# A hybrid decoder layer on one core: x and B of the SSD mixer turned by VectorE and DMA instead of TensorE

## The chip, the cores and the metric

The kernel runs on one core of a Trainium2 chip. The metric is the device time of one execution in microseconds (us). A comparison of this kernel can tell a difference of about 0.2%, some 5 us, from none.

## What is computed

One layer on 16 learned meta tokens and 2048 tokens of 1024 features, all in float32. `u`, `z`, `xBC` and `dt` are columns of one projection; x has 24 heads of 64 channels in 4 groups, B and C have 128 channels per group.

```python
def reference(x, meta, norm_mix_w, w_in, ...):
    h = concatenate([meta, x])
    hn = rms_norm(h, norm_mix_w)
    u, z, xbc, dt_raw = split(hn @ w_in)                 # 512, 1536, 2560, 24 columns
    y_pool = pool_mixer(u, pool_w, pool_scale)           # trailing means over 2, 4, 8, 16 tokens
    y_ssm = ssd_mixer(z, xbc, dt_raw, ...)
    h = h + concatenate([y_pool, y_ssm]) @ w_out
    h = h + square(relu(rms_norm(h, norm_ffn_w) @ w_ff1)) @ w_ff2
    return rms_norm(h, norm_f_w)[16:]

def ssd_mixer(...):                                      # per chunk of 128 tokens and group g
    x, B, C = silu(causal_dwconv(xbc))                   # width 4, over tokens
    y_diag = ((C @ B.T) * decay) @ (x * dt)
    state  = state * chunk_decay + B.T @ (decay_to_end * x * dt)
    y_off  = (C @ state_before) * exp(a_cs)
    y = (y_diag + y_off + d_skip * x) * silu(z)          # then a norm per group and ssm_norm_w
```

## The kernel before

The sequence is cut into 4 blocks of 512 tokens (`TB`). Block 0 splits each fp32 weight into a high and a low fp32r part (`high_part` on ScalarE, L541; `low_part`, L556, on VectorE in the mixer) and stores both in DRAM (`w_scr`); blocks 1 to 3 load them back. Every product is then three fp32r products. A block runs the input projection in items (`unit`, L1901), the mixer steps between them, and then the output projection. After the four blocks come the feed-forward products, from 1390 us to the end, which the change doesn't enter.

**Items.** An item is one tile of 128 channels by 512 tokens: per group g the tiles B (j=0), C (j=1) and three x tiles (j=2, 3, 4), then z: in block 0 three more tiles, in blocks 1 to 3 four pieces of one chunk each (`z_unit`, L1910). Last come four pool tiles. For each item TensorE makes the product into bank 0 or 1; ScalarE copies it out (`evac`, L1317); VectorE runs three convolution taps (`taps`, L2378), ScalarE a tanh, VectorE the SiLU product (`finish`, L2394), which writes `group_tile(g, j)` in feature order (channels on partitions). `evac(v)` waits until item v-2 is finished, and TensorE starts item v+2 only when `evac(v)` is done.

**Mixer steps.** Step q (16 in a block, four chunks c for each group) mixes group g while the items of group g+1 run; for the last group only one pool item runs in each step. In a step TensorE does: item n1, `y_transposes(q-2)`, `diagonal(q-1)` (L2023; it waits for `xw_ready(q-1)`), `slot1(q)`, `state(q-1)`, item n2, `y_offset(q)`. The mixer needs x and B of the chunk with tokens on partitions, so `slot1` (L1973) turns four 128x128 tiles on TensorE into bank 4 or 5 (L1985), ScalarE copies them to `xb` and `b_plain` or `b_both` (L1547, L1549), and GpSimd (`ty`, L1125) and VectorE (`xdt` L2583, `xw` L2587) read `xb`. VectorE's order in a step is: `y_finish`, `state_add` of the step before, taps of n1, in block 0 the low weight part of n1+2, the mask, the product with E, `xdt`, `xw`, low parts, the `finish` of two items, `yo`, in block 0 the low weight part of n2+2, taps of n2.

**Queues.** All DMAs are issued by SyncE in one written order. In the loop over n (L825) it issues, in block 0, the stores of the split weights of unit n-4 (which wait for the low part of that unit) and then the raw load of unit n; in blocks 1 to 3 it waits until unit n-4 or so is done and loads the two parts of unit n. Between them stand the store of the running totals (`store_sums`, L791) and the loads of their broadcasts (`load_sums`, L800), which ScalarE's exponentials need.

## Time and profile before

| | |
|---|---|
| median of 3 runs | 2673.69 us (2671.85 to 2674.07) |
| span of the profiled execution | 2674.7 us |
| busy TensorE, VectorE, ScalarE, GpSimd | 99%, 61%, 48%, 41% |
| granted TensorE clock, mean | 0.999 of full speed |

The span runs from the first to the last instruction and stands 1.0 us above the median, so a shift that is worked out in the span is applied to the median as it is. In the rows further down a timeline line has its start, its length (of all xcount instructions together), the engine and the source line, what is written and read, and in brackets the idle time before it with what ended it. "PE" is TensorE, "DVE" VectorE, "ACT" ScalarE, "POOL" GpSimd, "SPq" SyncE's queue.

### The profile page before, as it was taken

To read this page: it belongs to the slowest core of one execution; us is meant where nothing else is said; L and a number is where in the kernel's file an instruction comes from. 1 tells how busy PE (TensorE), PEld (TensorE's weight loads), DVE (VectorE), ACT (ScalarE), POOL (GpSimd) and SP (SyncE) were. 2 spreads that over 40 slices of the span, in tenths; PEclk is the share of its full clock that TensorE was granted. 3 is DMA by queue.
4 is the path that set the end of the run, shared out by engine and by line. 5 is a ranking of instruction groups with operands and counts; after the bars stand their busy time and mean duration, and the time that the engine had idled before them with its cause. 6 is when DMAs were issued, how large, how long until landed. Compare 5 with 4: busy or idle time off the path is not lost.

```text
span 2674.7 us, 37670 instructions
## 1 busy us (share of the span) xinstructions
PE 2654.5 (99%) x14058; PEld 2225.0 (83%) x14058; DVE 1636.3 (61%) x2204; ACT 1281.4 (48%) x2562; POOL 1091.7 (41%) x866
## 2 busy tenths in 40 slices
PE   8999999999999999999999999999999999999998
PEld 6788778888888888898888888888888888888887
DVE  6788714788136883367853576574445766666667
ACT  4577654666245672355734454555454322222223
POOL 2133440335003441023444688665554535353434
PEclk9999999999999999999999999999999999999999
DMA  9977676654646546555574555774445842423324
GB/s 327 299 255 244 237 247 223 251 181 172 220 174 245 194 160 236 190 215 181 188 267 142 200 197 203 259 259 154 152 151 207 309 145 96 164 103 126 118 95 157
DMA packets 224451, 531.14 MB, mean 199 GB/s; under 512 B 14074, under 2 KB 97022, under 8 KB 214798
## 3 DMA queue, kind: packets, MB, share of 16 engines
q1 hardware_dynamic: 224270, 528.74, 55.3%
q8 instruction: 112, 1.84, 0.3%
q14 instruction: 69, 0.57, 0.1%
HBM read 382.74 MB, written 145.95 MB: 198 GB/s over the span
## 4 chain that ended last, share of the span: by engine, by line
PE 95%; DMA 2%; SPq 1%; DVE 1%; issue 0%; POOL 0%; ACT 0%; POOLq 0%; ACTq 0%
PE bank L2257 23%; PE bank L2225 22%; PE bank L1832 21%; PE bank L1939 12%; PE bank L1919 7%; PE bank L2023 2%; PE bank L1985 1%; PE bank L2040 1%; PE bank L2003 1%; PE bank L2011 1%; DMA w_scr<-w_both 1%; DMA meta_w<-in_w_in 1%; PE bank L1991 1%; PE bank L1958 1%; DMA raw<-in_w_out 0%
## 5 line engine op out<-in xcount | busy, mean ns | idle before, releaser
L1832 PE MATMUL bank<-hnT_hi,w_ring 128*128 128x512 f32 x1152 | 369.4, 392 | 0.0
L2257 PE MATMUL bank<-w_first,T_hi 128*128 128x512 f32 x896 | 275.8, 389 | 0.0
L2387 DVE SCALAR_TENSOR_TENSOR acc<-pre,par,acc 128x512 f32<-128x512 f32 x240 | 211.6, 882 | 90.4 <-ACT pre L1345 84.6
L1832 PEld LDWEIGHTS bank<-hnT_hi,w_ring 128*128 128x128 f32 x1152 | 216.3, 188 | 44.5 <-ACT win_tmp L1474 0.5
L2742 DVE TENSOR_TENSOR acc_th<-bank,acc_th 128x512 f32<-128x512 f32 x224 | 150.0, 686 | 155.4 <-PE bank L2257 154.0
L2225 PE MATMUL bank<-T_hi,w_both 128*128 128x512 f32 x768 | 242.4, 389 | 0.5 <-DVE ff L2683 0.5
L1939 PE MATMUL bank<-w_ring,T_hi 128*128 128x512 f32 x768 | 239.0, 392 | 0.1
L1832 PE MATMUL bank<-hnT_lo,w_ring 128*128 128x512 f32 x576 | 224.5, 390 | 0.0
L2257 PEld LDWEIGHTS bank<-w_first,T_hi 128*128 128x128 f32 x896 | 168.2, 188 | 34.9
L1919 PE MATMUL bank<-w_ring,hnT_hi 128*128 128x384 f32 x768 | 196.0, 336 | 0.0
L1832 PE MATMUL bank<-hnT_hi,w_both 128*128 128x512 f32 x544 | 183.1, 408 | 2.3 <-ACT pre L1345 2.3
L2225 PE MATMUL bank<-b,w_both 128*128 128x512 f32 x768 | 179.5, 389 | 0.0
L2257 PE MATMUL bank<-T_hi 128*128 128x512 f32 x448 | 174.3, 389 | 0.0
L2257 PE MATMUL bank<-T_lo,T_hi 128*128 128x512 f32 x448 | 174.3, 389 | 0.0
L2257 PE MATMUL bank<-w_first,T_lo 128*128 128x512 f32 x448 | 174.3, 389 | 0.0
L2257 PE MATMUL bank<-T_hi,T_lo 128*128 128x512 f32 x448 | 174.3, 389 | 0.0
L2225 PEld LDWEIGHTS bank<-T_hi,w_both 128*128 128x128 f32 x768 | 144.1, 188 | 31.2 <-DVE ff L2683 1.3
L2225 PEld LDWEIGHTS bank<-b,w_both 128*128 128x128 f32 x768 | 144.0, 188 | 30.3 <-DVE ff L2675 0.5
L1939 PEld LDWEIGHTS bank<-w_ring,T_hi 128*128 128x128 f32 x768 | 142.5, 188 | 30.0 <-DVE y L2465 1.3
L1630 ACT ACTIVATE w_both<-w_sum 128x512 fp32r<-128x512 f32 x128 | 81.0, 633 | 172.5 <-PE bank L2225 138.9
L2225 PE MATMUL bank<-hnT_hi,w_both 128*128 128x512 f32 x512 | 163.1, 389 | 0.0
L1706 ACT ACTIVATE T_hi<-third 128x1024 fp32r<-128x1024 f32 x56 | 56.3, 1053 | 220.4 <-PE bank L2257 207.7
(315 smaller groups left out, 6315.2 us busy)
## 6 DMA issues: line engine op xcount, KB each, us to landing
w_ring<-w_scr SPq DMA_DIRECT2D x312, 512.0 KB, 4.3
T_scr<-stage SPq DMA_DIRECT2D x32, 1792.0 KB, 6.7
w_scr<-w_both SPq DMA_DIRECT2D x100, 512.0 KB, 4.3
pair_raw<-in_w_ff SPq DMA_DIRECT2D x36, 1024.0 KB, 5.6
third<-T_scr SPq DMA_DIRECT2D x28, 1024.0 KB, 4.9
pair_raw<-T_scr SPq DMA_DIRECT2D x28, 1024.0 KB, 4.9
sums<-sums_scr SPq DMA_DIRECT2D x64, 384.0 KB, 5.0
raw<-in_w_in SPq DMA_DIRECT2D x36, 512.0 KB, 6.4
```

What stands on the lines that cost most here:

```text
L1630: nc.scalar.activation(hi, left_source(g), ACT.Copy).then_inc(w1_hi, 1)
L1706: nc.scalar.activation(hi[:, k, :], t_raw[x % 2][:, k, :], ACT.Copy).then_inc(t_hi, 1)
L1832: mm = nc.tensor.matmul(bank[s][:, :], w[:, k, :], t[:, k, :], start=(k == 0 and j == 0), stop=(k == KT - 1 and j == 2))
L1919: mm = nc.tensor.matmul(bank[s][:, 0:GW].rearrange("p (u c) -> p u c", c=P), t[:, k, tok], w[:, k, :, :], start=(k == 0 and j == 0), stop= ...
L1939: mm = nc.tensor.matmul(bank[4 + t][:, :], a, w[:, kk, :], start=(u == 0 and kk == 0 and j == 0), stop=(u == 7 and kk == 1 and j == 2))
L1958: mm = nc.tensor.transpose(dst[:, t * P:(t + 1) * P], h[:, t, k * P:(k + 1) * P], ident[:, :])
L1985: mm = nc.tensor.transpose(bank[4 + q % 2][:, i * P:(i + 1) * P], group_tile(g, j)[:, cols], ident[:, :])
L2023: mm = nc.tensor.matmul(bank[6][rows, r * HEAD:(r + 1) * HEAD], E[:, r, rows], xdt[:, r * HEAD:(r + 1) * HEAD], start=True, stop=True, til ...
L2225: mm = nc.tensor.matmul(bank1(p, m), w[:, k, :], t[:, k, :], start=(m not in (2, 7, 3) and k == 0 and j == 0), stop=(m not in (1, 6, 5) an ...
L2257: mm = nc.tensor.matmul(bank[4 * half + t][:, :], a[:, k, tok], w[:, k, :], start=(SECOND[q % 7] not in GOES_ON and k == 0 and j == 0), st ...
L2387: ins = nc.vector.scalar_tensor_tensor(acc[:, s, 0:TB], pre[:, s, k:k + TB], w, acc[:, s, 0:TB], ALU.mult, ALU.add)
L2742: ins = nc.vector.tensor_tensor(dst, src, dst, ALU.add)
```

## The change

TensorE no longer turns x and B. `finish` of the tiles j = 0, 2, 3, 4 writes its SiLU product (for x into the scratch `pre`, for B into `group_tile(g, 0)`), waits for it, and then turns it with a VectorE transposition, which turns each 32x32 block in its place: x to `group_tile(g, j)`, B to `b_turn`, the space of `win_tmp`. ScalarE issues a store of each turned tile to `xt_scr` in DRAM, behind the `evac` of the item two later. SyncE loads each chunk back with four DMAs, one for each 32 partitions, in runs of 32 floats, which puts the blocks in token order in `xt[:, c, :]`. In blocks 1 to 3 chunks 0 and 1 of a group are asked for behind the load of unit 8(g+1), chunks 2 and 3 behind unit 8(g+1)+3; in block 0 one chunk each behind units 8(g+1)+5 to +8, and for the last group behind units 37, 38, 39 and again 39. VectorE, GpSimd and, in blocks 1 to 3, ScalarE wait for `xt_loaded[c]` where they waited for `xb_ready`.

```diff
                     g, j = divmod(n if b else n - 5, UNITS_G)          # SyncE, behind load(N0 + n)
+                    if g and b and j == 0:  load_tokens(b, g - 1, 0); load_tokens(b, g - 1, 1)
+                    elif g and b and j == 3: load_tokens(b, g - 1, 2); load_tokens(b, g - 1, 3)
+                    elif g and b == 0 and j < CH: load_tokens(b, g - 1, j)
...
+                            if b == 0 and d == 0 and 1 <= i < 4:
+                                load_tokens(b, GROUPS - 1, i - 1)
+                                if i == 3: load_tokens(b, GROUPS - 1, 3)
...
+                def load_tokens(b, g, c):
+                    xt_stored.wait(sp, b, 48 * (g + 1))
+                    b_stored.wait(sp, b, 16 * (g + 1))
+                    if b or g:                                          # the readers of this chunk's last use
+                        b0, q0 = (b, (g - 1) * CH + c) if g else (b - 1, STEPS - CH + c)
+                        xw_ready.wait(sp, b0, q0 + 1)
+                        ty_ready.wait(sp, b0, q0 + 1)
+                        if b0 == 0: state_ps.wait(sp, b0, q0 + 1)
+                    blocks = xt_scr[b, g, :, :, c * P:(c + 1) * P].rearrange(
+                        "t (i a) (j f) -> j a (t i) f", a=32, f=32)
+                    for j in range(4):
+                        sp.dma_start(xt[32 * j:32 * j + 32, c, :].rearrange("p (k f) -> p k f", f=32),
+                                     blocks[j]).then_inc(xt_loaded[c].sem, 16)
...
+                def store_turned(b, v):                                 # ScalarE, at the end of evac(b, v + 2)
+                    ...
+                    act.dma_start(xt_scr[b, g, j - 2 if j else 3], turn_tile(g, j)
+                                  ).then_inc(xt_stored.sem if j else b_stored.sem, 16)
...
-                        xb_ps.wait(act, b, q + 1)
-                        ...
-                        nc.scalar.activation(xb[:, :], bank[4 + q % 2][:, 0:GW], ACT.Copy
-                                             ).then_inc(xb_ready.sem, 1)
+                        if b:
+                            xt_loaded[c].wait(act, b, 64 * (g + 1))
+                            nc.scalar.activation(b_both[q % 2][:, 0, :], xt[:, c, GW:GW + P],
+                                                 ACT.Copy).then_inc(b_hi_ready.sem, 1)
...
-                    for i, j in enumerate((2, 3, 4, 0)):                # TensorE, slot1
-                        mm = nc.tensor.transpose(bank[4 + q % 2][:, i * P:(i + 1) * P],
-                                                 group_tile(g, j)[:, cols], ident[:, :])
...
+                        steps.link(nc.vector.scalar_tensor_tensor(dst, pre[:, s, 0:TB], 1.0,
+                                                                  acc[:, s, 0:TB], ALU.add, ALU.mult))
+                        if j == 0 and g:
+                            b_stored.wait(dve, b, 16 * g)
+                            sums_stored.wait(dve, b, 16 * GROUPS)
+                        nc.vector.transpose(turn_tile(g, j), dst).then_inc(up_out.sem, 1)
...
-                        xb_ready.wait(dve, b, q + 1)
+                        xt_loaded[c].wait(dve, b, 64 * (g + 1))
```


`zs`, the turned z of block 0, moves into the space of `h`, and the load of `h` in block 0 waits for `gated(15)` for that reason; B of block 0 is read straight from `xt` by `state`.

## Rows read from the trace of the kernel before

**Rows 1.** the page: the chain that ended last, shares by engine.

```profile
PE 95%; DMA 2%; SPq 1%; DVE 1%; issue 0%; POOL 0%; ACT 0%; POOLq 0%; ACTq 0%
```

**Rows 2.** groups by line: turning x and B; busy, mean | idle before.

```profile
L1985 PE MATMUL bank<-ident,F 128*128 128x128 f32 x256 | 41.7, 286 | 0.0
```

**Rows 3.** timeline of TensorE, block 1, step 2.

```profile
491.55 0.66 PE L1985 MATMUL bank<-ident,F 128*128 128x128 f32 x4
492.04 0.39 PE L1991 MATMUL bank<-F 128*128 128x128 f32 x2
```

**Rows 4.** timeline of VectorE, block 0: three linked taps, a copy, a contended finish.

```profile
69.28 2.32 DVE L2387 SCALAR_TENSOR_TENSOR acc<-pre,par,acc 128x512 f32<-128x512 f32 x3
89.90 0.68 DVE L2305 COPY F<-bank 128x512 f32<-128x512 f32 x1
...
152.74 1.50 DVE L2417 SCALAR_TENSOR_TENSOR F<-pre,acc 128x512 f32<-128x512 f32 x1
```

**Rows 5.** timeline, block 1, step 10: VectorE, ScalarE, TensorE.

```profile
613.42 1.29 DVE L2417 SCALAR_TENSOR_TENSOR F<-pre,acc 128x512 f32<-128x512 f32 x2
...
614.14 0.49 ACT L1329 ACTIVATE pre<-bank 128x384 f32<-128x384 f32 x1 [1.23 <-DVE F L2417]
...
616.62 0.52 PE L1919 MATMUL bank<-w_ring,hnT_hi 128*128 128x384 f32 x2
```

**Rows 6.** timeline, block 1, before its first step: ScalarE, SyncE's queue, TensorE.

```profile
450.86 0.49 ACT L1330 ACTIVATE acc<-bank 128x384 f32<-128x384 f32 x1
...
454.83 0.34 SPq L804 DMA_DIRECT2D sums<-sums_scr  x1
459.19 0.81 SPq L788 DMA_DIRECT2D w_ring<-w_scr  x2
...
465.06 0.47 PE L1832 MATMUL bank<-hnT_hi,w_ring 128*128 128x512 f32 x1
```

**Rows 7.** timeline, block 0, step 12: VectorE, SyncE's queue, TensorE.

```profile
268.06 1.21 DVE L562 TENSOR_TENSOR w_both<-raw,w_both 128x1024 fp32r<-128x1024 f32 x1
273.38 1.18 DVE L2583 TENSOR_TENSOR xdt<-xb,dtt 128x384 f32<-128x384 f32 x1
274.95 0.54 DVE L2587 TENSOR_TENSOR xw<-xb,dte 128x384 f32<-128x384 f32 x1
...
270.14 0.80 SPq L490 DMA_DIRECT2D raw<-in_w_out  x1
...
276.16 0.92 PE L2023 MATMUL bank<-xdt,E 128*64 128x64 f32 x24
...
285.21 0.92 PE L2023 MATMUL bank<-xdt,E 128*64 128x64 f32 x24
```

**Rows 8.** tile raw, 277 to 292 us: its DMAs, from issue to landing.

```profile
DMA to landing us min/median/max: 5.2/5.4/5.6
```

**Rows 9.** windows of 1 us: engines' busy us, granted clock, DMA share, GB/s.

```profile
13.00:14.00 1.00, 0.83 (x8) 0.59 (x6) 0.44 (x1) 1.00 (x3) 1.00 (x1) 1.00 1.20 220
25.00:26.00 1.00, 1.00 (x6) 0.84 (x5) 0.00 (x0) 0.00 (x0) 0.00 (x0) 1.00 1.10 351
...
281.00:282.00 1.00, 1.00 (x6) 0.84 (x5) 0.97 (x2) 1.00 (x5) 0.48 (x2) 1.00 0.91 252
```

**Rows 10.** block 0's first step: SyncE's queue, VectorE, TensorE; its raw load's landing.

```profile
101.46 0.57 SPq L490 DMA_DIRECT2D raw<-in_w_in  x1
...
107.08 0.55 DVE L2583 TENSOR_TENSOR xdt<-xb,dtt 128x384 f32<-128x384 f32 x1
...
112.16 0.92 PE L2023 MATMUL bank<-xdt,E 128*64 128x64 f32 x24
...
DMA to landing us min/median/max: 9.4/9.4/9.5
```

**Rows 11.** timeline of TensorE, and a window behind it, block 0.

```profile
79.69 0.47 PE L1832 MATMUL bank<-hnT_hi,w_both 128*128 128x512 f32 x1 [2.34 <-ACT pre L1345]
...
80.30:83.30 3.00, 3.00 (x9) 2.35 (x8) 2.93 (x5) 2.61 (x6) 0.00 (x0) 0.50 1.06 378
```

More of the change, by code:

```diff
@@ L256, in build @@
         b_both = [at(f"b_both{i}", [P, 2, P], h_at + 7168 + 1024 * i, F32R) for i in range(2)]
-        b_plain = at("b_plain", [P, 2, P], h_at + 9216)
+        zs = at("zs", [P, GW], h_at + 10240)
         t1_at = at("t1_at", [P, 4, TB], R0 + 65536)
@@ L355, in build @@
                        for c in range(CH)]
-        xb_ps = sig("xb_ps", STEPS)
+        b_stored = sig("b_stored", 16 * GROUPS, 0)
+        xt_stored = sig("xt_stored", 48 * GROUPS, 0)
+        xt_loaded = [sig(f"xt_then_w2_loaded{c}", 64 * GROUPS, 0) for c in range(CH)]
         zc_ps = sig("zc_ps", STEPS)
         z_late = sem("z_late")
-        xb_ready = sig("xb_ready", STEPS)
+        b_hi_ready = sig("p_hi_then_b_hi", STEPS, KT, 0)
         exp_ready = sig("exp_ready", STEPS)
@@ L399, in build @@
         split_loaded = [sem(f"split_loaded{i}") for i in range(3)]
-        w2_loaded = [sem(f"w2_loaded{i}") for i in range(5)]
+        w2_loaded = [xt_loaded[i].sem if i < CH else sem("w2_loaded4") for i in range(5)]
         w2_sum_ready, w2_hi, w2_lo = sem("w2_sum_ready"), sem("w2_hi"), sem("w2_lo")
@@ L749, in _ @@
                     meta_pair(j)
-                initial = [s for s in signals if s.start and s not in (state_ready, *sums_loaded)]
+                initial = [s for s in signals if s.start and s not in (state_ready, b_hi_ready, *sums_loaded)]
                 for j in range(4, POOL_PAIR):
@@ L828, in _ @@
                             meta_pair(POOL_PAIR + n - RING - 1)
+                        g, j = divmod(n if b else n - 5, UNITS_G)
+                        if g and b and j == 0:
+                            load_tokens(b, g - 1, 0)
+                            load_tokens(b, g - 1, 1)
+                        elif g and b and j == 3:
+                            load_tokens(b, g - 1, 2)
+                            load_tokens(b, g - 1, 3)
+                        elif g and b == 0 and j < CH:
+                            load_tokens(b, g - 1, j)
                         if n == (8 if b else 12):
@@ L857, in _ @@
                                 state_ps.wait(sp, b, STEPS)
+                                if b == 0:
+                                    gated.wait(sp, b, STEPS)
                                 sp.dma_start(h[:, :, :], x_in[0, b * TB:(b + 1) * TB, :].rearrange(
@@ L1121, in _ @@
                             inverse_root(b, rsy[:, :], ssy[:, :], ssy_ready, q, rsy_ready, 1)
-                        xb_ready.wait(pool, b, q + 1)
+                        xt_loaded[c].wait(pool, b, 64 * (g + 1))
                         gated.wait(pool, b, q)
-                        steps.link(nc.gpsimd.tensor_tensor(by_head(ty[:, :]), by_head(xb[:, :]),
+                        steps.link(nc.gpsimd.tensor_tensor(by_head(ty[:, :]), by_head(xt[:, c, 0:GW]),
                                                            per_head(dsk, 0, g), ALU.mult))
@@ L1315, in _ @@
                 steps = Steps(act, act_sem)
+                def store_turned(b, v):
+                    n = unit_of(b, v) if v >= 0 else None
+                    if n is None or n >= U_POOL or n % UNITS_G not in (0, 2, 3, 4):
+                        return
+                    g, j = divmod(n, UNITS_G)
+                    act.dma_start(xt_scr[b, g, j - 2 if j else 3], turn_tile(g, j)
+                                  ).then_inc(xt_stored.sem if j else b_stored.sem, 16)
                 def evac(b, v):
@@ L1321, in evac, with evacuate @@
                     up_out.wait(act, b, v - 1)
+                    evacuate(b, v, s, ps)
+                    store_turned(b, v - 2)
+                def evacuate(b, v, s, ps):
                     piece = piece_of(b, v)
@@ L1512, in _ @@
                             acsT_ps.wait(act, b, 1)
+                            b_stored.wait(act, b, 16)
                             nc.scalar.activation(acsT, bank[3][0:HEADS, :], ACT.Copy
@@ L2034, in state @@
                         xw_ready.wait(pe, b, q + 1)
-                        nc.tensor.matmul(bank[7][:, 0:GW], b_plain[:, q % 2, :], xw[:, :],
+                        xt_loaded[q % CH].wait(pe, b, 64 * (q // CH + 1))
+                        nc.tensor.matmul(bank[7][:, 0:GW], xt[:, q % CH, GW:GW + P], xw[:, :],
                                          start=True, stop=True).then_inc(state_ps.sem, 1)
@@ L2161, in after_mixer @@
                     def after_mixer(t):
-                        if t == 0:
-                            xb_ready.wait(pe, b, STEPS)
-                        elif t == 2:
+                        if t == 2:
                             gated.wait(pe, b, STEPS)
@@ L2423, in finish @@
                     up_evac.wait(dve, b, v + 1)
+                    b_stored.wait(dve, b, 16 * GROUPS)
                     E_ = TB + 16
@@ L2582, in _ @@
                             state_ps.wait(dve, b, q)
-                        nc.vector.tensor_tensor(by_head(xdt[:, :]), by_head(xb[:, :]),
+                        nc.vector.tensor_tensor(by_head(xdt[:, :]), by_head(xt[:, c, 0:GW]),
                                                 per_head(dtt, c, g), ALU.mult)
```

42 lines of the change are left out of this document (25 added, 17 removed).

## The prediction

> **What bounds the kernel now.** I read the page first: TensorE is busy for 99% of the span, as the table above has it, and makes 95% of the chain that ended last [rows 1]. So the time is the sum of what TensorE issues, plus the few places where it waits, and any other engine counts only where it makes TensorE wait. Second, the groups by line: the 256 transpositions of x and B are busy for 41.7 us with no idle time before them [rows 2]. Busy time of one instruction overlaps with the next on TensorE, so it is not what removing it gives; the timeline is: from the start of the four of L1985 to the start of what follows is 492.04 - 491.55 = 0.49 us [rows 3]. Third, the timelines of the places where data now has to come by another way, to see how long before TensorE's need it would arrive. I say below how much room each has.
>
> **What the change removes.** 64 steps (16 in each of 4 blocks) of 0.49 us on TensorE, all on the path: 64 x 0.49 = 31.4 us. That is the whole gain, and it is there only while TensorE stays the last to arrive. ScalarE loses the copy to `xb` in every step and `b_plain` in block 0; it is not the bound, so this is worth nothing by itself.
>
> At this point the Trainium skill speaks for a larger gain: "VectorE: DVE Perf Modes", section "The three transpose paths", gives 390 ns for one 128x128 transposition on TensorE, which would be 100 us for 256; here four of them take 0.49 us [rows 3], and the row decides. The same section recommends TensorE for a full 128x128 transposition, since VectorE turns only within 32x32 blocks; what that leaves to the DMAs is priced next, from rows.
>
> **What it adds on VectorE.** 64 transpositions of 128x512, each linked behind its SiLU product. No transposition stands in the trace. The nearest row is a copy of that shape, 0.68 us; three linked taps take 2.32 us where three alone would take about 3 x 0.68, so a link costs some 0.13 us [rows 4]. A turned `finish` is then 0.8 us longer than before. Bounds: 0.3 us (half a copy, no link) and 1.6 us (the 1.50 us of a finish that ran beside GpSimd [rows 4]). I take 0.8.
> In blocks 1 to 3 this bites in the third step of each of the groups 0 to 2 (9 steps). VectorE has no pause there from `y_finish` to the two `finish` at 613.42; ScalarE's `evac` of a z piece waits for the first of them (1.23 us) and ends at about 615.0, and TensorE starts two pieces later at 616.62 [rows 5]: 1.6 us of room. Between the two ends TensorE loses two `slot1`, 1.0 us, and VectorE gains 0.8 us: room -0.2. With a semaphore's travel I take 0.3 us of waiting each, 9 x 0.3 = 2.7 us (0 to 9).
>
> **What it adds on ScalarE.** 64 DMA issues behind an `evac`, 0.3 to 0.4 us each as for SyncE's of that size [rows 6]; the copy that falls away frees about as much. Nothing waits for them: `evac(v)` has already waited for item v-2. In the start of block 0 the DMAs are the limit, and a 256-KB store costs its share there, some 0.7 us of waiting.
>
> **What a chunk load costs.** A chunk is 4 DMAs of 512 runs of 128 bytes, 128 runs for each of the 16 DMA engines. Runs of 1 KB move at 351 GB/s, which is 47 ns for a run on one engine; runs of 512 bytes at 252 GB/s, 33 ns. The microsecond that holds the load of 1024 runs of 96 bytes falls to 220 GB/s [rows 9]; if it holds all of them they took 10 ns each. The line through 1 KB and 512 bytes gives 22 ns at 128 bytes. I take 17 ns, 2.2 us for a chunk. Bounds: 0.7 us (bytes alone) and 4.2 us (a run as dear as one of 512 bytes), with the rival below beyond that. To this come 4 x 0.4 us of issue on SyncE. In blocks 1 to 3 most of it lies in the stretch of the z pieces, where SyncE only waits.
>
> The Trainium skill has a rule against this part: "DMA: Bandwidth & Descriptors", section "Specifications", says that line rate wants at least 512 bytes and that below this the DMA reads, modifies and writes. The row of the 96-byte runs doesn't show runs dearer than those of 512 bytes; were each of them twice as dear, the sum would be that of the first rival's far end.
>
> **Where chunks arrive late, block 0, last group.** SyncE issues chunk 0 only behind the raw load of unit 37 (270.14), which itself stands behind the stores that wait for the low part of unit 33, done at 269.3. That raw load lands 5.4 us after its issue at 270.14 [rows 7, 8], at 275.5; the chunk's data is queued behind it: 2.2 us more, 277.8, that is 8.6 us after the low part. VectorE wanted it at 273.38 and needs 2.1 us from there to the end of `xw` (275.49); so `xw` ends at about 279.9. TensorE's `diagonal(12)` started at 276.16 [rows 7], now 0.5 us earlier: a wait of 4.3 us. Behind the waiting VectorE stand `yo` and the low part of unit 34, and that low part is what SyncE's next store waits for, and behind it stands chunk 1. So there is a loop: low part, 8.6 us, chunk, 2.1 us, `xw`, 1.7 us, next low part: 12.4 us for a step, where TensorE wants 9.05 - 0.49 = 8.6 us (9.05 from 276.16 to the next `diagonal` at 285.21, less 0.49). It is closed twice (chunks 1 and 2; chunk 3 is asked for together with 2): 2 x 3.8 = 7.6. Together 11.9 us. Besides, an idle of 2.34 us is followed by a stretch at a granted clock of 0.50 from 80.3 to 83.3 us [rows 11], that is 1.2 GHz for 3 us: some 1.5 to 1.7 us lost. Within the loop this hides in the wait; once it comes out at the end. Last group: 13.6 us (8 to 19).
>
> **Block 0, first step.** SyncE comes out of the wait for the sums late: the raw load in front of chunk 0 is issued at 101.46 and lands 9.4 us later, at 110.9; the chunk at 113.1. VectorE wanted it at 107.08, and `diagonal(0)` started at 112.16 [rows 10]: with `xw` at 114.3 TensorE waits 2.6 us. VectorE is then 6 us behind in a stretch in which it has almost no pause (two items with taps and two low parts in a step), so low parts of the next units are late too; following the order up to unit 14 I get 4.8 us in all (2 to 9). The other groups of block 0 have two items and so a longer step, in which I see the chunks come in time; 0.5 us for VectorE's longer `finish`.
>
> **Blocks 1 to 3, first step.** The store of the last x tile of group 0 is issued after the `evac` that ends at 451.35 (450.86 + 0.49), and I take 2.7 us for it to land, half of [rows 8], as it is half as large. SyncE, which waits for it, then issues 8 DMAs (3.5 us) and only then the store and the loads of the sums: the first, before at 454.83, comes at about 460.1, and the load of unit 9, which waited for TensorE until 459.19, at 460.5. TensorE needs that unit at 465.06 [rows 6], now 0.5 earlier. I give that load 4.6 us to land (5.4 for the larger one of [rows 8]), so near 465.1: 0.5 us each, 1.5 us (0 to 6). In all other groups the stores land before the z pieces are done, and the chunks have 5 to 10 us.
>
> **Sum.** -31.4 + 0.7 (stores at the start) + 13.6 (last group, block 0) + 4.8 + 0.5 (other groups, block 0) + 2.7 (VectorE, blocks 1 to 3) + 1.5 (their first steps) = -7.6 us. Block 0 loses 12 us net, the other three win 19. The span of 2674.7 becomes 2667.1, and the median 2673.7 becomes 2666.1.
>
> **Rivals.**
> 1. *Short runs are dear (slower).* The place is the chunk's time in SyncE's queue. Each us more of it costs TensorE about 7 us: three times in the last group of block 0, once in its first step, and in the first steps of blocks 1 to 3 once two chunks take longer than the 6 us between their issue and the load of unit 9. From 3.3 us for a chunk (26 ns a run) the change loses. At 4.2 us (33 ns, as for 512 bytes): -7.6 + 7 x 2.0 = +6.4, 2680. At twice that, 8.4 us, it is +36, 2710, and more where block 0's DMAs fill up. For it: no run of 128 bytes in the trace. Against: the 96-byte runs.
> 2. *VectorE is the bound in blocks 1 to 3.* A turned `finish` of 1.5 us instead of 0.8: the 9 steps cost 1.0 instead of 0.3 us, and block 0 another 2: -7.6 + 8.3 = +0.7, 2674. For it: GpSimd runs beside VectorE in most of these steps, and the order there has no pause. Against: `mask` in block 0 comes 0.5 us earlier, since ScalarE no longer copies `xb` in front of `zs`.
> 3. *The chunks are in time.* If a chunk costs 1 us and lands 7.2 us after the low part, the last group costs 2.9 + 2 x 2.4 = 7.7 with no loss of clock, the first step 2.5, blocks 1 to 3 about 1: -31.4 + 0.7 + 7.7 + 2.5 + 0.5 + 1 = -19, 2655.
>
> **Chances.** Forecast 0.45, its own range 2660 to 2673; rival 1 0.20; rival 2 0.15; rival 3 0.20. The range goes from 2652 (below rival 3: no wait in blocks 1 to 3) to 2686 (a chunk of 5 us); only the dear half of rival 1 and mishaps outside lie beyond. About 0.2%, 5.3 us, is what a measurement can tell: faster means below 2668.3. From the forecast 0.33, from rival 3 0.19, from the others 0.02: 0.54. Same: 0.12 of the forecast, 0.10 of rival 2, 0.05 of rival 1: 0.27. Slower: 0.19.
>
> **What would show it.** In the profile after: no L1985 group, and in an undisturbed step of blocks 1 to 3 a distance of 0.49 us less from one `diagonal` to the next. Transpositions of VectorE at about 0.7 us. TensorE's idle time in the list of waits: about 10 us more in block 0's last group, ended by VectorE's `xw`, with VectorE's `xdt` waiting for the DMAs of `xt`; three waits of 4 us there, 12.4 us apart; one near the first step. Blocks 1 to 3 each 6 us shorter. I am wrong if chunks land much more or less than 2.2 us behind the raw load in front of them, if the idle time of blocks 1 to 3 is above 10 us, or if the loop of the last group doesn't show.

## The result, and the profile after

The changed kernel takes 2692.5 us (median of 4 runs, 2691.25 to 2696.14) against 2673.9 us for the kernel before on the same chip: a ratio of 1.0074 (95% interval 1.006 to 1.0088). It is 0.7% slower, where 0.3% faster was forecast and the range ended at 2686.

First the page of the changed kernel: busy times, the DMA packets, and the chain that ended last by engine.

```profile
span 2690.0 us, 37628 instructions
...
PE 2645.0 (98%) x13802; PEld 2209.0 (82%) x13802; DVE 1659.2 (62%) x2268; ACT 1253.6 (47%) x2482; POOL 1119.9 (42%) x866
...
DMA packets 368837, 564.71 MB, mean 210 GB/s; under 512 B 150266, under 2 KB 233214, under 8 KB 359182
...
PE 82%; DMA 2%; SPq 2%; DVE 2%; issue 1%; POOL 0%; ACT 0%; POOLq 0%; ACTq 0%; DVEq 0%
```

The profiled span grew by 15.3 us (2674.7 to 2690.0; the medians are 18.6 us apart, and what follows accounts for the spans), while TensorE's busy time fell from 2654.5 to 2645.0 us. So TensorE stood idle for 45.0 instead of 20.2 us, 24.8 more. The mean granted clock fell from 0.999 to 0.994; summed over windows of 1 us, the time lost to a clock below full speed is 16.87 instead of 3.63 us, 13.2 more. What is left, 15.3 - 24.8 - 13.2 = -22.7 us, is the work removed. The packets under 512 bytes went from 14,074 to 150,266. The chain answers [rows 1]: TensorE has 82% of it instead of 95%, and SyncE's queue and VectorE have 2% each instead of 1%.

What TensorE waited for in the changed kernel (engine, line, what it waited for: us in total, times, longest):

```profile
PE bank L1885 <- DMA w_ring<-w_scr: 12.5, 4, 3.9
PE bank L2059 <- DVE T_lo L2544: 7.7, 3, 3.3
...
PE bank L1885 <- ACT pre L1401: 2.8, 2, 1.4
PE bank L2071 <- issue: 2.4, 1, 2.4
```

(The row left out, 5.8 us in the first microseconds, stands in both kernels.) The second row is the wait of the last group of block 0 that was forecast; the `diagonal` behind it needs `xw`, and `T_lo` is only VectorE's instruction next to it. The fourth is block 0's first step. The first and third rows were not forecast in this size: weights of blocks 1 to 3 that come late. The third names `pre` because ScalarE's instruction ended last. But the weights of that item land at 477.67 and TensorE goes on at 477.80, and in the kernel before it started the same item at 465.06 [rows 6], before that instruction of ScalarE (465.57 to 466.17) was done.

Where it happens is seen best in a table worked out from the timelines: the start of `diagonal` (L2023 before, L2071 after) in chosen steps of both kernels, and the difference.

```
block step   before     after    difference
  0    0     112.16    115.25     +3.09
  0    1     126.69    132.51     +5.82
  0   11     267.07    268.65     +1.58
  0   15     303.32    314.82    +11.50
  1    0     476.71    489.42    +12.71
  1    1     490.70    508.71    +18.01
  1   15     659.85    673.09    +13.24
  2    0     824.00    838.11    +14.11
  2    1     837.99    857.48    +19.49
  2   15    1007.13   1021.87    +14.74
  3    0    1171.33   1187.17    +15.84
  3    1    1185.32   1205.73    +20.41
  3   15    1354.47   1370.16    +15.69
```

Between these places the difference falls: by 4.24 us from step 1 to 11 of block 0, and by 4.77, 4.75 and 4.72 us from step 1 to 15 of the blocks 1 to 3. That is 18.48 us in 52 steps, 0.36 us in a step: the gain. It is lost at three kinds of places: block 0's first two steps, its last four, and the first two steps of each of the blocks 1 to 3. The last kind alone costs more than the other two together.

### The profile page after: what moved, and what is told of

The parts are those of the page before. It is cut to its first block, busy times and chain, and to the rows that moved or that the text cites. A ratio compares the mean times of both kernels' runs of the same rounds, so it can differ in the third digit from the quotient of the medians.

```text
span 2690.0 us, 37628 instructions
## 1 busy us (share of the span) xinstructions
PE 2645.0 (98%) x13802; PEld 2209.0 (82%) x13802; DVE 1659.2 (62%) x2268; ACT 1253.6 (47%) x2482; POOL 1119.9 (42%) x866
## 4 chain that ended last, share of the span: by engine, by line
PE 82%; DMA 2%; SPq 2%; DVE 2%; issue 1%; POOL 0%; ACT 0%; POOLq 0%; ACTq 0%; DVEq 0%
PE bank L2304 23%; PE bank L2272 22%; PE bank L1885 13%; PE bank L1992 12%; PE bank L1972 7%; PE bank L2071 1%; DMA w_ring<-w_scr 1%; SPq L832 1%; PE bank L2089 1%; PE bank L2051 1%; PE bank L2039 1%; PE bank L2059 1%; PE bank L2011 1%; DMA w_scr<-w_both 0%; PE bank L2004 0%
## 5 line engine op out<-in xcount | busy, mean ns | idle before, releaser
L1885 PE MATMUL bank<-hnT_hi,w_ring 128*128 128x512 f32 x1152 | 373.8, 396 | 15.3 <-DMA w_ring<-w_scr 12.5
L1885 PEld LDWEIGHTS bank<-hnT_hi,w_ring 128*128 128x128 f32 x1152 | 218.6, 190 | 62.6 <-ACT pre L1401 13.2
L2434 DVE SCALAR_TENSOR_TENSOR acc<-pre,par,acc 128x512 f32<-128x512 f32 x240 | 202.8, 845 | 81.7 <-ACT pre L1401 75.9
L1992 PEld LDWEIGHTS bank<-w_ring,T_hi 128*128 128x128 f32 x768 | 142.8, 188 | 28.7
L2783 DVE TENSOR_TENSOR T_lo<-third,T_hi 128x1024 fp32r<-128x1024 f32 x56 | 160.6, 2869 | 4.8 <-ACT T_hi L1759 4.7
L1238 POOL TENSOR_TENSOR w_both<-w_sum,w_both 128x512 fp32r<-128x512 f32 x64 | 86.8, 1357 | 180.0 <-ACT w_both L1683 179.6
```

Source lines behind the costliest of these rows:

```text
L1238: nc.gpsimd.tensor_tensor(lo, left_source(g), hi.bitcast(F32), ALU.subtract).then_inc(w1_lo_pool, 1)
L1885: mm = nc.tensor.matmul(bank[s][:, :], w[:, k, :], t[:, k, :], start=(k == 0 and j == 0), stop=(k == KT - 1 and j == 2))
L1992: mm = nc.tensor.matmul(bank[4 + t][:, :], a, w[:, kk, :], start=(u == 0 and kk == 0 and j == 0), stop=(u == 7 and kk == 1 and j == 2))
L2434: ins = nc.vector.scalar_tensor_tensor(acc[:, s, 0:TB], pre[:, s, k:k + TB], w, acc[:, s, 0:TB], ALU.mult, ALU.add)
L2783: nc.vector.tensor_tensor(lo[:, k, :], t_raw[x % 2][:, k, :], hi[:, k, :].bitcast(F32), ALU.subtract).then_inc(t_lo, 1)
```

## What a step gains

The forecast was 0.49 us a step, from the start of the four transpositions to the start of what follows [rows 3]. The timeline of TensorE from one `diagonal` on, block 1, step 2, before:

```profile
502.08 0.92 PE L2023 MATMUL bank<-xdt,E 128*64 128x64 f32 x24
502.93 0.66 PE L1985 MATMUL bank<-ident,F 128*128 128x128 f32 x4
503.42 0.39 PE L1991 MATMUL bank<-F 128*128 128x128 f32 x2
503.56 0.78 PE L2040 MATMUL bank<-xw_both,b_both 128*128 128x384 f32 x3
504.19 0.52 PE L1919 MATMUL bank<-w_ring,hnT_hi 128*128 128x384 f32 x2
```

and the same step after:

```profile
519.71 0.92 PE L2071 MATMUL bank<-xdt,E 128*64 128x64 f32 x24
520.56 0.49 PE L2039 MATMUL bank<-F 128*128 128x128 f32 x2
520.82 0.79 PE L2089 MATMUL bank<-xw_both,b_both 128*128 128x384 f32 x3
521.45 0.51 PE L1972 MATMUL bank<-w_ring,hnT_hi 128*128 128x384 f32 x2
```

The transpositions are gone and their 0.49 us with them. But the two matmuls behind them, which took 0.14 us from start to start (503.42 to 503.56), now take 0.26 (520.56 to 520.82), and from `diagonal` to the item the way is 1.74 instead of 2.11 us: 0.37 are gained. Undisturbed steps gain mostly 0.40 to 0.43 us in block 0 and 0.29 to 0.41 in blocks 1 to 3; only 0.09 is gained from step 14 to 15 of each of these three blocks, which no row here explains. Over all 52 steps of the table it is 0.355, and 64 x 0.355 = 22.7 us, not 31.4: as much as the work removed above. (The expectations below were written with 0.39.)

## Blocks 1 to 3: what the two waits are

The timeline of SyncE's queue in the changed kernel, around the first steps of block 1:

```profile
464.10 4.04 SPq L832 DMA_DIRECT2D xt<-xt_scr  x8
468.18 1.41 SPq L807 DMA_DIRECT2D sums_scr<-win_tmp  x4
470.76 0.34 SPq L815 DMA_DIRECT2D sums<-sums_scr  x1
471.21 0.84 SPq L799 DMA_DIRECT2D w_ring<-w_scr  x2
...
475.51 12.52 SPq L832 DMA_DIRECT2D xt<-xt_scr  x8
488.07 0.49 SPq L815 DMA_DIRECT2D sums<-sums_scr  x1
488.61 0.43 SPq L881 DMA_DIRECT2D hT_scr<-hT  x1
```

and TensorE's two waits there, the window in the second of which the clock falls, and a window in the first eight chunk loads (columns as in [rows 9]):

```profile
477.80 0.47 PE L1885 MATMUL bank<-hnT_hi,w_ring 128*128 128x512 f32 x1 [1.37 <-ACT pre L1401]
501.15 0.47 PE L1885 MATMUL bank<-hnT_hi,w_ring 128*128 128x512 f32 x1 [3.85 <-DMA w_ring<-w_scr]
...
503.00:506.00 3.00, 3.00 (x8) 2.31 (x8) 0.83 (x2) 0.00 (x0) 0.00 (x0) 0.52 0.99 380
...
467.00:468.00 1.00, 1.00 (x8) 1.00 (x7) 0.43 (x1) 0.54 (x2) 0.00 (x0) 1.00 0.90 141
```

Up to the second load of eight the issues come as forecast. Block 1 starts 11.56 us late, so 470.76 is 459.2 on the scale of before (forecast 460.1), and unit 9's weights are asked for at 471.21, that is 459.65 (forecast 460.5). The load takes 6.1 us to land where 4.6 was taken, and so TensorE waits 1.4 instead of 0.5 us. The runs of 128 bytes are cheap for the DMA engines: while nothing else moves they run at 141 GB/s at a share of 0.90, and the 4096 packets of these two chunks took 12.9 ns each in the packet records, against the 17 ns taken and the 33 ns of the upper bound.

The second load of eight, chunks 2 and 3, was not worked through in the prediction. The first eight issues took 4.04 us, these take 12.52 us, with single issues of 4.97 and 3.83 us among them. Behind them stand the 2-MB store of `hT` and the weights of units 12 and 13; before, the weights of unit 12 were asked for at 464.87, now at 489.14 (477.58 on the old scale). TensorE waits 3.9 us for them, and then runs 3.4 us at the clock level of 1.2 GHz (the window at 0.52; it is 2.4 GHz before and behind): 1.7 us more. The three blocks have first waits of 1.37, 1.40 and 1.64 us, second waits of 3.85, 3.91 and 3.11, and each 1.7 us of lost clock: 20.4 us together, where the forecast had 1.5.

Two theories for the second wait: it is the place in SyncE's order (theory A), or the DMA engines are full there in any order (theory B).

### Chunks 2 and 3 two units later

```diff
-                        elif g and b and j == 3:
+                        elif g and b and j == (5 if g < GROUPS else 3):
                             load_tokens(b, g - 1, 2)
                             load_tokens(b, g - 1, 3)
```

> The changed kernel, with one thing moved: in blocks 1 to 3 SyncE issues the loads of chunks 2 and 3 of groups 0 to 2 behind the weights of unit 8(g+1)+5 instead of 8(g+1)+3. Theory A (place in the queue): in the changed kernel the eight DMAs of that pair held SyncE from 475.5 to 488.0 us, and the weights for which TensorE waited 3.9, 3.9 and 3.1 us in the second steps of blocks 1, 2 and 3 stood behind them; each wait was followed by some 1.7 us lost to a granted clock of 0.50. Then these waits go: 3 x (3.6 + 1.7) = 16 us, 2692.5 becomes 2676. Theory B (the DMA engines are full there whatever the order): within 3 us of 2692.5.

Measured: 2696.3 us, ratio 1.0081 (1.0068 to 1.0093). Theory A, as I had it, falls; theory B's range is missed too, by 0.8 us. SyncE's queue and TensorE in this kernel:

```profile
473.41 7.99 SPq L799 DMA_DIRECT2D w_ring<-w_scr  x4
481.57 15.01 SPq L832 DMA_DIRECT2D xt<-xt_scr  x8
...
507.59 0.98 PE L1972 MATMUL bank<-w_ring,hnT_hi 128*128 128x384 f32 x2 [5.70 <-DMA w_ring<-w_scr]
```

The eight loads now hold SyncE for 15.0 us and the wait stands one step later, 5.7 us long. The stop goes wherever the pair goes.

### Chunk loads in long runs

```diff
-                        sp.dma_start(xt[32 * j:32 * j + 32, c, :].rearrange("p (k f) -> p k f", f=32),
-                                     blocks[j]).then_inc(xt_loaded[c].sem, 16)
+                        sp.dma_start(xt[32 * j:32 * j + 32, c, :],
+                                     xt_scr[b, g, c, 32 * j:32 * j + 32, :]
+                                     ).then_inc(xt_loaded[c].sem, 16)
```

> The changed kernel, but a chunk load takes as many bytes in as many DMAs at the same places as runs of 2 KB from xt_scr (so x and B are not in token order: this part of the computation is left wrong). Theory C (the short runs, 512 of them in a DMA, are what holds SyncE's queue and makes the chunks late): the second waits of blocks 1 to 3 go (-16 us) and the last group of block 0 loses some 3 us less: 2673. Theory A (the place behind other transfers, whatever the runs): a chunk costs 1.1 us of DMA time less, each wait shrinks by no more than that: 2692.5 - 8 = 2684 or above.

This kernel leaves out the token order of x and B. Measured: 2679.9 us, ratio 1.0017 (1.0008 to 1.0027): 12.6 us less, nearer to theory C. SyncE's queue at the same place:

```profile
469.37 3.92 SPq L832 DMA_DIRECT2D xt<-xt_scr  x8
473.32 0.42 SPq L815 DMA_DIRECT2D sums<-sums_scr  x1
```

Eight DMAs with as many bytes behind the same transfers take 3.92 us to issue, not 12.52. The place is the same and so are the bytes, so it is the number of packets, 512 in a DMA instead of 32. TensorE's second waits are 1.7, 1.8 and 1.7 us. The half of theory C that speaks of block 0 is wrong: its last group waits 3.7, 1.5 and 2.0 us, as long as in the changed kernel.

Counting the packets of SyncE's queue (those of all DMAs issued since the queue was last empty, less those whose end is in the records) shows how full it is when an issue takes long:

```
kernel         issue at   outstanding when it starts   it takes
changed         475.91        1347                      0.79
changed         476.75        1765                      4.97
changed         481.76        1766                      0.68
changed         482.61        2192                      3.83
long runs       474.76         968                      0.44
spread          499.70        1766                      0.49
spread          500.24        2222                      3.50   (sums, 128 packets)
```

From 440 to 1390 us, in blocks 1 to 3, no issue of any kernel here ends with more than 2270 packets outstanding, and in the first steps of block 1 before the change the count stays below 1150. But 2270 is not the size of a buffer. In block 0, where a raw load is 1024 packets of 512 bytes, issues of 0.5 us end with some 2500 outstanding, before the change as well (0.44 us at 106.70, from 1542 to 2523). And some issues take long on fewer, or don't end when there is room again: the one of 3.83 us ends when only 630 are left, and in the kernel with chunk 1 later (below) one that starts with 1226 takes 4.10 us. So long issues come with many packets outstanding; what exactly is full then, and when it lets go, stays open.

The load of the DMA engines alone doesn't explain the long issues. During the issue of 4.97 us they are busy (284 to 427 GB/s in windows of 1 us), but during the one of 3.83 us they run dry, while SyncE has yet to issue the loads for which TensorE will wait (a window in each, columns as in [rows 9]):

```profile
480.00:481.00 1.00, 1.00 (x6) 0.84 (x5) 0.53 (x3) 1.00 (x4) 0.84 (x1) 1.00 1.00 406
...
486.00:487.00 1.00, 1.00 (x6) 0.84 (x5) 1.00 (x3) 0.00 (x0) 0.29 (x1) 1.00 0.18 27
```

The Trainium skill, "Perfetto Trace Analysis", section "DMA Instruction — HWDGE (DVE, Sync)", says that the profile shows of a DMA the time in which its descriptors are made, and that the engines may begin before that ends "if more descriptors are generated than fit in the descriptor buffer". It names no size. The long issues agree with such a buffer, but the counts give it no size.

### Chunks 2 and 3 apart, behind other weights

Theory D: SyncE stops when too many packets are outstanding on its queue. Then chunks have to be asked for where few are.

```diff
                         if g and b and j == 0:
-                            load_tokens(b, g - 1, 0)
-                            load_tokens(b, g - 1, 1)
-                        elif g and b and j == 3:
+                            if g > 1:
+                                load_tokens(b, g - 2, 3)
+                                load_tokens(b, g - 1, 0)
+                                load_tokens(b, g - 1, 1)
+                        elif g and b and j == 7:
+                            load_tokens(b, g - 1, 2)
+                        elif g == GROUPS and b and j == 3:
                             load_tokens(b, g - 1, 2)
                             load_tokens(b, g - 1, 3)
...
                             for c in range(1 if b else CH):
                                 load_sums(b, 0, c)
+                            if b:
+                                load_tokens(b, 0, 0)
+                                load_tokens(b, 0, 1)
```

> The changed kernel with other places for the chunk loads of blocks 1 to 3: chunks 0 and 1 of group 0 behind the store and first load of the sums instead of ahead of them, chunk 2 of groups 0 to 2 behind unit 8(g+1)+7, chunk 3 behind unit 8(g+2), each alone. The late pair has shown that moving both chunks by two units only moves the wait (5.7, 5.6, 5.2 us instead of 3.9, 3.9, 3.1). Theory D (the number of packets that SyncE's queue takes): a chunk is 2048 packets of 128 bytes; eight DMAs of 512 packets behind 877 packets of weights and sums stopped SyncE for 4.97 us in one issue with about 1770 packets outstanding, and the next weights were asked for that much later. One chunk at a time on a queue of under 400 packets passes, so both waits of each block go, with the clock that they cost: 3 x (1.4 + 3.6 + 1.7) = 20 us: 2672. Theory B (the DMA engines are full, whatever the order): the waits stay above 1.5 us with their loss of clock: 2682 or more.

Measured: 2676.3 us, ratio 1.0008 (1.0000 to 1.0017); 16.2 us less than the changed kernel, where 20 were expected. The second waits are gone in all three blocks, with their loss of clock: 3 x (3.6 + 1.7) = 15.9 us. The first waits stay, at 1.17, 1.21 and 1.54 us: chunks 0 and 1, now behind the sums, still stand ahead of unit 9. Theory B falls: the DMA engines are as full as before (a share of 1.0 and more in nearly all windows of 1 us from 478 to 502 us), and TensorE doesn't wait for the weights.

The kernel isn't quite what its expectation says. Only chunk 2 stands alone. Chunks 0 and 1 of group 0 are still asked for together, with 128 packets outstanding, and take 5.4 us to issue; chunk 3 stands with chunks 0 and 1 of the next group, twelve DMAs in 15.2 us from 504.88 on, waits between them included. SyncE still has single issues of up to 3.5 us (the sums behind chunk 2 in the table), and no weights are late by them. So the place counts beside the number: what matters is that nothing urgent stands behind a long issue.

### Chunk 1 behind the weights of unit 13

> The version with block 0 on TensorE and the new places in blocks 1 to 3, with chunk 1 of group 0 behind unit 13 instead of ahead of unit 9. The four waits that are left (0.55, 0.35, 1.50, 1.06 us) stand at unit 9 and its neighbours; with 2048 packets fewer ahead of it, unit 9's weights land some 2 us earlier: the waits go, 2660.6 - 3 = 2657.5. If SyncE stands in chunk 1 behind unit 13 with about 750 packets before it, the weights of unit 14 come late and the time is 2660 or above.

```diff
                                 load_tokens(b, 0, 0)
-                                load_tokens(b, 0, 1)
...
+                        elif g == 1 and b and j == 5:
+                            load_tokens(b, 0, 1)
                         elif g and b and j == 7:
```

Measured: 2674.1 us, ratio 0.9999 (0.9990 to 1.0007), against 2660.6 us for the same kernel without this edit (below). The first branch of the expectation was wrong, and the second came true. It is strong evidence for theory D:

```profile
467.20 10.54 SPq L832 DMA_DIRECT2D xt<-xt_scr  x4
477.78 2.70 SPq L815 DMA_DIRECT2D sums<-sums_scr  x1
...
488.77 0.79 PE L2108 MATMUL bank<-xw_both,b_both 128*128 128x384 f32 x3 [1.73 <-DVE yo L2682]
490.50 0.98 PE L1982 MATMUL bank<-w_ring,hnT_hi 128*128 128x384 f32 x2 [0.95 <-DMA w_ring<-w_scr]
```

A single chunk, asked for with some 750 packets outstanding, holds SyncE for 10.5 us; with 128 outstanding, two chunks held it for 5.4 us in the kernel with chunks 2 and 3 apart. (Part of the 2-MB store of `hT` is among the 750, so the bytes outstanding differ as well.) Chunk 1 is then late itself, so VectorE's `yo` and TensorE's `state` wait, and the weights behind it are late too. The first waits at unit 9 did go, as expected, and waits of 1.7 to 1.8 and 0.7 to 1.0 us and the clock came in their place, three times.

## Block 0

The last group behaves as the prediction has it. VectorE, SyncE's queue and TensorE in the changed kernel, answering [rows 7]:

```profile
279.29 0.56 DVE L2642 TENSOR_TENSOR xdt<-xt,dtt 128x384 f32<-128x384 f32 x1 [4.23 <-DMA xt<-xt_scr]
...
281.34 1.21 DVE L569 TENSOR_TENSOR w_both<-raw,w_both 128x1024 fp32r<-128x1024 f32 x1
...
270.89 0.80 SPq L737 DMA_DIRECT2D w_scr<-w_both  x2
...
272.68 2.94 SPq L832 DMA_DIRECT2D xt<-xt_scr  x4
282.57 0.81 SPq L737 DMA_DIRECT2D w_scr<-w_both  x2
...
294.60 0.81 SPq L737 DMA_DIRECT2D w_scr<-w_both  x2
...
280.46 0.73 PE L2059 MATMUL bank<-ident,y 128*128 128x128 f32 x3 [3.32 <-DVE T_lo L2544]
```

`xdt` waits 4.2 us for the chunk, the low part stands behind it (281.34 to 282.55), SyncE's next stores follow it at 282.57, and so the loop turns: 11.7 and 12.0 us from store to store, where 12.4 was forecast. TensorE waits 3.3, 1.7 and 2.7 us and loses 1.7 us of clock twice: 11.1 us.

### TensorE turns in block 0, the change in blocks 1 to 3 alone

```diff
+                    if b == 0:                                          # TensorE, slot1
+                        if q > 1:
+                            xt_loaded[(q - 2) % CH].wait(pe, b, 64 * ((q - 2) // CH + 1))
+                        for i, j in enumerate((2, 3, 4, 0)):
+                            mm = nc.tensor.transpose(bank[4 + q % 2][:, i * P:(i + 1) * P],
+                                                     group_tile(g, j)[:, cols], ident[:, :])
...
+                            nc.scalar.activation(xt[:, c, :], bank[4 + q % 2][:, :], ACT.Copy
+                                                 ).then_inc(xt_loaded[c].sem, 64)
...
-                        if ct is None or j == 1:
+                        if b == 0 or ct is None or j == 1:
```

> Only blocks 1 to 3 have the change; in block 0 TensorE turns x and B as before and ScalarE copies them into xt. By the account of the traces block 0 pays 5.1 us in its first steps, 11.1 in its last group, 1.0 in its start and 0.5 in its output projection, and wins 16 x 0.39 = 6.2: 11.5 us net. So 2692.5 - 11.5 = 2681. If the waits of block 0 only hid others, the time stays above 2686.

Measured: 2678.8 us, ratio 1.0015 (1.0006 to 1.0023). Block 0 loses 13.7 us net by the change; 11.5 were expected. No wait of TensorE above 0.4 us is left in block 0's mixer, and the waits of blocks 1 to 3 are as in the changed kernel (1.3 to 1.5 and 3.7 to 4.3 us).

### Chunks asked for earlier in block 0

```diff
-                        elif g and b == 0 and j < CH:
+                        elif g and b == 0 and j < CH and n != 13:
                             load_tokens(b, g - 1, j)
+                        if b == 0 and n == 12:
+                            load_tokens(b, 0, 0)
+                        if b == 0 and n >= 34:
+                            load_tokens(b, GROUPS - 1, n - 34)
...
-                            if b == 0 and d == 0 and 1 <= i < 4:
-                                load_tokens(b, GROUPS - 1, i - 1)
-                                if i == 3:
-                                    load_tokens(b, GROUPS - 1, 3)
+                            if b == 0 and d == 0 and i < 2:
+                                load_tokens(b, GROUPS - 1, i + 2)
```

> The changed kernel with other places for the chunk loads of block 0: chunk 0 of group 0 ahead of the store of the sums, chunks 0 to 3 of the last group behind units 34 to 37. If the place behind the raw load is what makes them late, the wait of 2.4 us in the first step and the three of 3.3, 1.7 and 2.7 us in the last group go with the loss of clock behind them (1.7 + 3.4): 5.1 + 11.1 = 16 us: 2676. If VectorE's longer finish or the stores on the DMA engines are what makes block 0 late, 5 us go at most: 2687.

Measured: 2681.8 us, ratio 1.0032 (1.0019 to 1.0044): 10.8 us less than the changed kernel. In the last group the three waits of 7.7 us become one of 0.46 and one of 0.31 (for `zs`): that loss was the place of the loads. In the first steps the loss stays, though chunk 0 comes in time:

```profile
107.82 0.45 SPq L497 DMA_DIRECT2D raw<-in_w_in  x1
108.37 7.85 SPq L832 DMA_DIRECT2D xt<-xt_scr  x4
...
118.00 1.12 SPq L497 DMA_DIRECT2D raw<-in_w_in  x1
...
112.75 0.47 PE L1887 MATMUL bank<-hnT_hi,w_both 128*128 128x512 f32 x1 [0.87 <-DVE w_both L569]
121.55 0.47 PE L1887 MATMUL bank<-hnT_hi,w_both 128*128 128x512 f32 x1 [2.45 <-DVE w_both L569]
```

The loads of chunk 1 hold SyncE for 7.85 us, as those of chunk 0 did in the changed kernel (7.75 us at 103.12), and stores and the next raw weights stand behind.

### The same without VectorE's turn of x

> The changed kernel with the early places of block 0 and without VectorE's transposition of the x tiles (x is left unturned within its blocks). With the early places chunk 0 came in time, yet TensorE still waited 0.9 and 2.5 us for low weight parts in block 0's first steps. If VectorE's own work is what makes these low parts late, the waits go: 2681.8 - 5 = 2677 or less. If it is SyncE, which stood 7.85 us in the four loads of chunk 1 (108.4 to 116.3) ahead of the next raw weights, they stay: 2680 to 2683.

```diff
-                        if ct is None or j == 1:
+                        if ct is None or j:
```

Measured: 2680.3 us, ratio 1.0025 (1.0016 to 1.0034), 1.4 us less, within what the two samples scatter. TensorE waits 1.6 and 1.6 us for low parts in the first steps instead of 0.9 and 2.5. VectorE's turn isn't the main cause there. That SyncE's 7.85 us are it fits, but no run took them alone away, so this stays argued.

### Both sets of places

> The two sets of places together. If the losses are of the places alone, both sums go: 2692.5 - 20 - 16 = 2656, 0.7% below the kernel before; what is left of 64 x 0.39 = 25 us is then lost to the stores at the start (1) and what waits remain. If one only hides the other, above 2665.

Measured: 2667.2 us, ratio 0.9973 (0.9963 to 0.9983). Faster than the kernel before, and 11 us above the forecast. Of the sums, 16 and 11 us are there (2692.5 - 16.2 - 10.8 = 2665.5): the gains add up within the scatter, though the time is above the 2665 from which the expectation would have said that one loss hides the other. The forecasts for each were too large, by the waits that stayed.

## VectorE

### Without the turn of x

> The changed kernel without VectorE's transposition of the 12 x tiles of a block (48 of 64; x is left unturned within its 32x32 blocks, all else is the same). If VectorE bounds nothing in blocks 1 to 3 (my reading of the trace after: no wait of TensorE in the third steps), only block 0's first steps and last group can win: 2690 to 2692. If VectorE is a bound (the second rival of the prediction), 8 us or more go: 2684.

The edit is the one line of the kernel above, on the changed kernel. Measured: 2692.3 us, ratio 1.0069 (1.0053 to 1.0084), the time of the changed kernel. The turn itself costs nothing where it is. The groups of VectorE's instructions in the changed kernel show its size (busy, mean ns | idle before):

```profile
L2476 DVE STREAM_TRANSPOSE F<-pre 128x512 f32<-128x512 f32 x48 | 34.2, 712 | 1.7
...
L2476 DVE STREAM_TRANSPOSE win_tmp<-F 128x512 f32<-128x512 f32 x16 | 11.4, 711 | 0.6
```

0.71 us, where 0.7 was taken from the copy of [rows 4].

### The turn of x twice

```diff
+                        if j:
+                            steps.link(nc.vector.transpose(turn_tile(g, j), dst))
                         nc.vector.transpose(turn_tile(g, j), dst).then_inc(up_out.sem, 1)
```

> The same version (block 0 on TensorE, new places), but VectorE turns each x tile of blocks 1 to 3 twice (the second gives the same result): 0.8 us more in each of 36 finishes. If VectorE has room of at least 1.6 us in the third steps, as the absence of any wait there after the change says, the time stays at 2661 to 2663. If it stood at its bound, as the prediction had it (room -0.2 us), 9 third steps cost 1.6 us each: 2675.

Measured: 2683.7 us, ratio 1.0034 (1.0021 to 1.0046), 23 us above the same kernel with one turn. My expectation of room falls. TensorE around the third step of group 1 in block 1:

```profile
554.15 0.79 PE L2069 MATMUL bank<-s_both,c_both 128*128 128x384 f32 x3 [0.34 <-POOL s_both L1160]
...
562.03 0.80 PE L2107 MATMUL bank<-xw_both,b_both 128*128 128x384 f32 x3 [1.33 <-DVE yo L2683]
```

Two finishes of 0.8 us more come out as 1.33 + 0.34 = 1.67 us of waiting, and nearly so in each of the 9 third steps (14.3 us in all, 12.0 for VectorE and 2.3 for GpSimd). So in the third steps all of the added time shows: the room there is about zero with one turn, as the prediction worked out (-0.2 us). That a wait of 0.3 us followed from -0.2 was the part that did not come true. Of the rest, three waits of 1.5 us (4.6 in all) stand before the first steps of blocks 1 to 3, for VectorE's `dte`, where group 0 is turned; four to six us are not placed.

## The version that is faster than both

> Block 0 as before the change (TensorE turns, ScalarE copies to xt), blocks 1 to 3 with the change and the new places: 2678.8 - 20 = 2659 if theory D holds; 48 x 0.39 = 19 us below the kernel before would be 2655.

It is the kernel with TensorE's turn in block 0 and the spread chunk loads in blocks 1 to 3, both diffs above. Measured: 2660.6 us (2659.7 to 2663.7), ratio 0.9953 (0.9940 to 0.9967), 1.2% below the changed kernel. Its page and the first rows of what TensorE waited for:

```profile
PE 2636.4 (99%) x13866; PEld 2205.0 (83%) x13866; DVE 1646.4 (62%) x2252; ACT 1261.6 (47%) x2498; POOL 1116.1 (42%) x866
...
PE bank L1873 <- DVE F L2348: 5.9, 1, 5.9
PE bank L1894 <- DMA w_ring<-w_scr: 3.1, 3, 1.5
```

TensorE is busy for 18.1 us less than before. 48 x 0.355 = 17.0 of these are the gain of the steps; the rest is no more than the 1.7 us of slow clock of [rows 11], which this execution hadn't. 3 us of waits for weights are left of 15.

## Why the prediction was wrong, point by point

- *What bounds the kernel.* Right: everything that counted was time in which TensorE waited, or its clock behind a wait.
- *The removal, -31.4 us.* Mis-sized: -22.7, since 0.12 us of the 0.49 come back in the two matmuls behind, and a little more in some steps. With the true value the forecast sum is +1.1 us: this alone takes away the forecast gain. The 390 ns that the prediction quotes from the Trainium skill stand in "The three transpose paths" for bf16, where the tiles here are fp32.
- *VectorE's turn, 0.7 us and a link.* Right in size (0.71), and the room of about zero in the third steps as well. The term of 2.7 us was nothing.
- *ScalarE's stores, and 0.7 us at the start.* Nothing waits for the issues (0.33 us each). At the start `diagonal(0)` is 3.09 us late with a wait of 2.39 right before it, which leaves 0.7. That this is the forecast number is luck: `diagonal(0)` starts anywhere from 108.3 to 112.2 us in the four profiled kernels here that store nothing in block 0 (chunk 1 later 108.3, the kernel faster than both 109.5, TensorE turning in block 0 109.9, the turn twice 111.5) and in the kernel before (112.2), so the scatter of the start is larger than the term.
- *The price of a run.* 12.9 ns where 17 were taken; the Trainium skill's rule on runs below 512 bytes ("DMA: Bandwidth & Descriptors", "Specifications") doesn't show here, as packets of 512 bytes took 28.7 ns beside them (96 packets, the store of the sums) and 29.8 ns on average over the execution, most of them raw loads. The first rival had the right sign and the wrong mechanism: it wanted short runs dear for the DMA engines, and its figure of 6 us between two chunks and unit 9's load went by that. They are dear in number, for SyncE.
- *Block 0, last group, 13.6 us.* Mechanism and size right: 11.1 us, three waits and a loop of 12 us. The waits, 3.3, 1.7 and 2.7 us, were forecast at 4, the lost clock once instead of twice.
- *Block 0, first step, 4.8 us.* Size right (2.4 + 1.0 + 1.7 of clock = 5.1). The reason was only half of it: with chunk 0 in time the loss stays, so the agreement is luck in part.
- *Blocks 1 to 3, first steps, 1.5 us.* This is the step that failed: 20.4 us, 15.3 of them waits, where the prediction's own sign of being wrong was 10. From the last step of one block to the last of the next the loss grew by 1.7, 1.5 and 1.0 us, where each block was to win 6. The prediction followed chunks 0 and 1 past the sums and unit 9, and said of the others that SyncE only waits where they stand. Chunks 2 and 3 are issued behind unit 11, with 900 packets of weights and sums outstanding, ahead of the store of `hT` and units 12 and 13. Their eight issues were priced as 0.4 us each from issues with few packets outstanding [rows 6]; behind those 900 they took 12.5 us, and with 32 packets in a DMA instead of 512, at the same place, 3.9 us.
- *The sum.* -22.7 + 0.7 + 5.1 + 11.1 + 20.4 = +14.6 against +15.3 in the spans. Of the 0.7 us between, 0.5 are longer waits for GpSimd's low parts in block 0's output projection.

## What to carry to other kernels

Count a DMA's packets as well as its bytes. In this kernel an issue stopped SyncE for up to 5.3 us once many packets were outstanding, and with it all that stood behind it in its order; so ask for short runs where little is outstanding, and let nothing urgent stand right behind them. And take the gain of removed TensorE work from the starts of what stands around it on both sides, since its neighbour may take part of it back.

## What was not expected of the hardware

- With many packets outstanding on its queue a single issue of SyncE took up to 5.3 us (4.97 in the changed kernel, from 1765 outstanding), while with fewer most take 0.3 to 0.8 us. In blocks 1 to 3 no issue ended with more than 2270 outstanding, in block 0 some ended with over 2500.
- 4096 packets of 128 bytes moved at 12.9 ns each, at up to 141 GB/s, less than half the time of a packet of 512 bytes (29.8 ns on average).
- In the changed kernel each wait of TensorE of 2.4 to 3.9 us came with 3.4 us at 1.2 GHz (1.7 us lost). In the other kernels some waits of 3.3 to 4.3 us came with 6.8 us at that level, and so did each of the three waits of 5.2 to 5.7 us of the late-pair kernel. A wait of 1.67 us in block 0 had no drop behind it, and one of 1.04 us at 40 us had one of 10.2 us; of the other kernels two show such a drop there, two one of 3.4 us, and the rest none.
